# Every third modulation chunk of the attention calls sent to the buffers of the down weights

## The reference, cut to what matters

```python
for i in range(DEPTH):
    mod_lat = jax.nn.silu(c) @ w_ada[i] + b_ada[i]
    mod_ctx = jax.nn.silu(c_ctx) @ w_ada[i] + b_ada[i]
    sh1, sc1, g1, sh2, sc2, g2 = [m[:, None, :] for m in jnp.split(mod_lat, N_MOD, axis=-1)]
    ...
    attn = windowed_gqa_with_context(q, k, v, kc, vc, sink[i])
    four = fourier_mix(u, w_fourier[i])
    mix = jnp.concatenate([attn, four], axis=-1) @ w_out[i]
    x_mid = x + g1 * rmsnorm(mix, norm_post_mix[i])
    hf = modulate(rmsnorm(x_mid, norm_pre_ffn[i]), sh2, sc2)
    x = x_mid + g2 * rmsnorm(swiglu(hf, w_gate[i], w_up[i], w_down[i]), norm_post_ffn[i])
```

## Time and profile before

| what | before |
|---|---|
| median of three runs | 2457.35 us (2454.23 to 2459.2) |
| the profiled execution | 2455.65 us, its span 2453.8 us |
| PE busy, share of the span | 95% |
| chain that ended last: PE, DMA | 84%, 4% |
| mean DMA rate over the span | 160 GB/s |
| first call (latent, layer 0, 12 chunks) | 122.77 to 169.40 us |
| second call (context, layer 0, 12 chunks) | 182.10 to 225.08 us |
| third call (latent, layer 1, 14 chunks) | 740.23 to 792.21 us |

### The profile page before, as it was taken

One profiled execution on the slowest core, in us unless ns is written; L12 is line 12 of the kernel. 1 busy time (PEld: TensorE's weight loads), 2 busy tenths in 40 slices (PEclk: granted clock), 3 DMA queues, 4 the chain that ended last, 5 costly groups with the idle time before them and its releaser, 6 DMA issues.

```text
span 2453.8 us, 47218 instructions
## 1 busy us (share of the span) xinstructions
PE 2341.4 (95%) x19072; PEld 2069.9 (84%) x19072; DVE 1452.5 (59%) x2300; ACT 1031.2 (42%) x1614; POOL 301.2 (12%) x242
## 2 busy tenths in 40 slices
PE   6988999999998899999999999999999998999998
PEld 3855899899974799789998888899899888989997
DVE  1053366666625566676677654666766667555765
ACT  2153454444334433343346434533533455435433
POOL 0000000100000000000005426200000035336000
PEclk9999999999999999999999999999999998999999
DMA  6156545445426555355432223655444332125542
GB/s 273 69 206 241 192 177 181 180 181 178 148 86 241 189 189 190 115 201 189 173 120 104 87 71 123 225 184 186 170 179 181 119 137 87 70 88 183 203 179 103
DMA packets 65511, 392.50 MB, mean 160 GB/s; under 512 B 7264, under 2 KB 7392, under 8 KB 28000
## 3 DMA queue, kind: packets, MB, share of 16 engines
q1 hardware_dynamic: 64224, 383.81, 42.9%
q10 hardware_dynamic: 864, 5.17, 0.5%
q0 software_dynamic: 288, 1.57, 0.2%
HBM read 389.48 MB, written 1.05 MB: 159 GB/s over the span
## 4 chain that ended last, share of the span: by engine, by line
PE 84%; DMA 4%; DVE 4%; issue 3%; POOL 3%; ACT 2%; SPq 0%; POOLq 0%; DVEq 0%; ACTq 0%
PE ps L2118 19%; PE ps L2075 12%; PE ps L2076 11%; PE ps L2077 11%; PE ps L2120 10%; PE ps L2203 5%; DMA ring_a<-in_wa 3%; POOL t_lo L598 3%; PE ps L2218 2%; PE ps L2537 2%; PE ps L2678 1%; DMA work<-in_wa 1%; PE ps L1999 1%; PE ps L2023 1%; PE ps L2233 1%
## 5 line engine op out<-in xcount | busy, mean ns | idle before, releaser
L2118 PE MATMUL ps<-h_parts,w_hi 128*128 128x512 f32 x2000 | 711.7, 398 | 1.6 <-DVE w_lo L1341 1.6
L2120 PE MATMUL ps<-h_parts,w_lo 128*128 128x256 f32 x2000 | 561.6, 281 | 0.0
L2118 PEld LDWEIGHTS ps<-h_parts,w_hi 128*128 128x128 f32 x2000 | 376.0, 188 | 89.2 <-DVE w_lo L1341 2.4
L2120 PEld LDWEIGHTS ps<-h_parts,w_lo 128*128 128x128 f32 x2000 | 378.0, 189 | 0.0
L1341 DVE TENSOR_TENSOR w_lo<-ring_a,w_hi 128x1024 fp32r<-128x1024 f32 x308 | 363.3, 1221 | 12.7 <-ACT w_hi L692 12.5
L2075 PE MATMUL ps<-hid_hi,d_hi 128*128 128x256 f32 x1232 | 349.0, 283 | 0.0
L2076 PE MATMUL ps<-hid_lo,d_hi 128*128 128x256 f32 x1232 | 348.8, 283 | 0.0
L2077 PE MATMUL ps<-hid_hi,d_lo 128*128 128x256 f32 x1232 | 348.6, 283 | 0.0
L725 ACT ACTIVATE sg<-sg 128x256 f32<-128x256 f32 x130 | 54.4, 418 | 649.2 <-DVE sg L1396 649.2
L692 ACT CAST w_hi<-ring_a 128x1024 fp32r<-128x1024 f32 x308 | 305.6, 1040 | 7.8 <-DMA ring_a<-in_wa 7.8
L1396 DVE TENSOR_REDUCE sg<-ps 128x256 f32<-128x512 f32 x130 | 89.9, 691 | 299.9 <-PE ps L2120 299.8
(11 more groups left out here) (330 smaller groups left out, 3871.2 us busy)
## 6 DMA issues: line engine op xcount, KB each, us to landing
ring_a<-in_wa SPq DMA_DIRECT2D x282, 1024.0 KB, 4.8
ring_d<-in_wd SPq DMA_DIRECT2D x154, 512.0 KB, 5.2
work<-in_wa SPq DMA_DIRECT2D x6, 1024.0 KB, 22.3
work<-in_small POOLq DMA_DIRECT2D x2, 768.0 KB, 4.7
c<-in_c ACTq DMA_DIRECT2D x1, 1190.0 KB, 10.7
work<-in_c ACTq DMA_DIRECT2D x1, 1088.0 KB, 5.0
x<-in_x ACTq DMA_DIRECT2D x1, 1024.0 KB, 15.2
work<-in_ctx ACTq DMA_DIRECT2D x1, 1024.0 KB, 19.7
```

The costliest lines, as they stand in the source:

```text
L2118: nc.tensor.matmul(out, w_hi[:, f % 2, part, k, :], h_parts[:, k], start=(k == 0), stop=False, skip_group_check=True)
L2120: mm = nc.tensor.matmul(out[:, 1, :], w_lo[:, f % 2, part, k, :], h_hi[:, k, :], start=False, stop=(k == KD - 1), skip_group_check=True)
```

## The change

Of the chunks of `L0` and `L1`, every third one (index 2, 5, 8, ... within its group) is loaded into `ring_d`, both of its slots together, which are 1 MB; the others go through `ring_a` as before. That makes 8 of the 24 chunks of `L0` and 4 of the 14 of `L1`; the last two of `L1` stay in `ring_a`. The chunks of `ring_a` are renumbered for it. Two semaphores are added: `third_loaded` says that such a chunk has landed, `third_used` that it has been used. SP loads in the order of use: two chunks to `ring_a`, one to `ring_d`, and so on, where chunk `g` waits for the use of chunk `g - 3`. Before the first one of layer 1, SP waits until the down weights of the first two feed-forward calls have been used (`d_used` at `2 * FT`). Before the first down weights of calls 0 and 2, SP waits for the last third chunk of that layer. PE's `ada(g)` reads the chunk from `ring_d` and counts on `third_used`; ACT's `ada(b)` waits on `third_used` where the last chunk of its batch is a third one. No arithmetic changes.

```diff
@@ -307,6 +307,7 @@
         a_loaded = [sem("a_loaded0"), sem("a_loaded1")]
         d_loaded = [sem("d_loaded0"), sem("d_loaded1")]
         a_used, d_used = sem("a_used"), sem("d_used")
+        third_loaded, third_used = sem("third_loaded"), sem("third_used")
         early_loaded = [sem(f"early_loaded{i}") for i in range(ADA_EARLY)]
         x_loaded, xc_loaded, h2_part = sem("x_loaded"), sem("xc_loaded"), sem("h2_part")
         vec_loaded, c2_loaded, const_loaded, small_loaded, out_stored = (
@@ -410,6 +411,9 @@
             n += count
         assert n == LAYERS * NMOD // 2 and ada_from["M00"] >= NMOD // 2 and ada_from["B1"] >= NMOD // 2 + ADA_FIRST
 
+        in_thirds = {"adaL0": 0, "adaL1": 2 * ADA_STEP0 // 3}
+        thirds = {"adaL0": 2 * ADA_STEP0 // 3, "adaL1": ADA_STEP1 // 3}
+
         def ada_stage(name):
             return (f"ada{name}", A_ADA + ada_from[name], dict(ada_parts)[name], None)
 
@@ -430,7 +434,7 @@
         chunk0, n = {}, 0
         for name, _, count, _ in stages:
             chunk0[name] = n
-            n += count
+            n += count - thirds.get(name, 0)
 
 
         tile0, first0, n, m = {}, {}, 0, 0
@@ -453,7 +457,15 @@
 
         def ada_chunk(g):
             name = [m for m, _ in ada_parts if ada_from[m] <= g][-1]
-            return chunk0[f"ada{name}"] + g - ada_from[name]
+            i = g - ada_from[name]
+            return chunk0[f"ada{name}"] + i - ((i + 1) // 3 if f"ada{name}" in thirds else 0)
+
+        def third_chunk(g):
+            for name in in_thirds:
+                i = g - ada_from[name[3:]]
+                if 0 <= i < 3 * thirds[name] and i % 3 == 2:
+                    return in_thirds[name] + i // 3
+            return None
 
         def early_chunk(g):
 
@@ -522,8 +534,32 @@
                     sp.wait_ge(d_used, d - 1)
                 sp.dma_start(ring_d[:, slot].rearrange("p a b -> p (a b)"), src).then_inc(d_loaded[slot], 16)
 
+            def load_third(src, used):
+                if used is not None:
+                    sp.wait_ge(third_used, used)
+                sp.dma_start(ring_d[:, :].rearrange("p a b c -> p (a b c)"), src).then_inc(third_loaded, 16)
+
+            def load_thirds(name, first, count):
+                c0, n0 = chunk0[name], in_thirds[name]
+                load_a(c0, c0 % 2, wa[first])
+                load_a(c0 + 1, (c0 + 1) % 2, wa[first + 1])
+                if n0:
+                    sp.wait_ge(d_used, 2 * FT)
+                load_third(wa[first + 2], n0 or None)
+                with sp.Fori(0, thirds[name] - 1) as n:
+                    for u in range(2):
+                        load_a(n * 2 + (c0 + 2 + u), (c0 + u) % 2,
+                               wa[bass.ds(n * 3 + (first + 3 + u), 1)].rearrange("a p n -> (a p) n"))
+                    load_third(wa[bass.ds(n * 3 + (first + 5), 1)].rearrange("a p n -> (a p) n"), n + (n0 + 1))
+                for i in range(3 * thirds[name], count):
+                    c = c0 + i - thirds[name]
+                    load_a(c, c % 2, wa[first + i])
+
             for name, first, count, call in stages:
                 c0 = chunk0[name]
+                if name in in_thirds:
+                    load_thirds(name, first, count)
+                    continue
                 if call is None:
                     i = 0
                     if c0 == 0:
@@ -545,6 +581,8 @@
                 d0, dd = call * FT, ffns[call][0] * FT
                 load_a(c0, c0 % 2, wa[first])
                 load_a(c0 + 1, (c0 + 1) % 2, wa[first + 1])
+                if call in (0, 2):
+                    sp.wait_ge(third_used, in_thirds[f"adaL{call // 2}"] + thirds[f"adaL{call // 2}"])
                 load_d(d0, d0 % 2, wd[dd], wait=call > 0)
                 load_a(c0 + 2, c0 % 2, wa[first + 2])
                 load_d(d0 + 1, (d0 + 1) % 2, wd[dd + 1], wait=call > 0)
@@ -823,6 +861,8 @@
                 u, last = b % 2, BATCHES[b + 1] - 1
                 if early_chunk(last) is not None:
                     act.wait_ge(ada_early, early_chunk(last) + 1)
+                elif third_chunk(last) is not None:
+                    act.wait_ge(third_used, third_chunk(last) + 1)
                 else:
                     act.wait_ge(a_used, ada_chunk(last) + 1)
                 nc.scalar.copy(ada_rows[:, u, :], ps[:, 4 + u, 0:T]).then_inc(ada_row, 1)
@@ -1982,11 +2022,14 @@
 
             def ada(g):
 
-                b, n = batch_of(g), early_chunk(g)
+                b, n, third = batch_of(g), early_chunk(g), third_chunk(g)
                 u, i, last = b % 2, g - BATCHES[b], BATCHES[b + 1] - 1
                 if n is not None:
                     pe.wait_ge(early_loaded[n], 16)
                     tiles, done = early[:, n], ada_early
+                elif third is not None:
+                    pe.wait_ge(third_loaded, 16 * (third + 1))
+                    tiles, done = ring_d, third_used
                 else:
                     c = ada_chunk(g)
                     chunk_here(c, c % 2)
```

## The result

The changed kernel takes 2440.78 us (median of four runs, 2439.74 to 2444.25); the kernel before, with one more run beside it, 2455.84 us. The two medians are 15.1 us apart. The ratio on record is 0.9927, 95% interval 0.9915 to 0.9939: some 18 us, and by the interval 15 to 21, so the medians stand at its lower end. A second set of five runs, with its own runs of before beside it, gave 2441.14 us and 0.9929 (0.9916 to 0.9943). The forecast was 2436.0 us, 21.3 us faster; the range, 2431 to 2446, holds the result.

A forecast was written before the change was run, and what follows sets the result against it. PE's 19.9 us of waits for chunks, bound by the turnover of two buffers' slots, plus clock cost, were the stock. Savings of 3.0 + 11.3 + 7.0 = 21.3 us gave 2434.3 profiled, 2436.0 us as median; range 2431 to 2446.

The forecast's parts named there:

- Rival A: Attention calls: DMA engines deliver less than 422 GB/s; 16.1 us saved, 2441 us, or 2446 if the clock falls; chance 0.17.
- Rival B: First and third calls: softmax chain replaces the wait, they give half, 1.5 and 3.5 us; 2441 us; chance 0.06.
- the sum had 6.9: Second call, second way of reckoning: 9.1 us of waits less three staying at about 0.75 us give 6.9.
- the other 4.3 us: Second call: three low-clock stretches of about 1.45 us each vanish, 4.3 us together; lost if the clock still falls.
- First call, 3.0 forecast: First attention call: 2.04 us saved over five steps and 0.96 behind them, 3.0 us, leaving no wait for chunks.
- third call, 7.0 forecast: Third attention call: 6.10 us saved over five steps and 0.93 at 787.27, 7.0 us; supply still enough.
- the step with one chunk at 4.48 us: Latent calls: a step with one chunk lasts 4.48 us without waits, read from 144.25 to 148.73.
- The steps with two chunks: First call: a step with two chunks takes 5.45 us without waits, 5.79 less its wait of 0.34.
- Second call, 11.3 forecast: Second attention call: DMA engines become the bound; it ends at 213.8 instead of 225.08, saving 11.3 us.
- the price of a chunk, 2.49 us: Supply with three buffers: engines move 422 GB/s, so a chunk takes 2.49 us and three take 7.46.
- C: SP's in-order queue: a wait for a third chunk holds up loads behind it, 2457 us stands; chance 0.03.
- D: Instruction blocks queue behind weights on the DMA engines and stall PE; 2466 us at 3 us each; chance 0.03.

The follow-up runs named there:

- e1_floor: Changed kernel with one modulation chunk loaded per layer and used for all, 36 of 38 loads left out: 2435.95 us, ratio 0.9904.
- e2_sinks_after: Changed kernel with ACT doing exponentials and sink of the first head, then of the second, instead of both exponentials, then both sinks: 2438.32 us, ratio 0.9916.
- e4_five: Changed kernel with five chunk buffers in place of three: 2436.75 us, ratio 0.9910.
- e5_five_sinks: Changed kernel with five chunk buffers and ACT doing each head's exponentials and sink together: 2427.38 us, ratio 0.9876.
- e6_four: Changed kernel with four chunk buffers in place of three: 2434.75 us, ratio 0.9908.

## Why the prediction was right, and where its terms were off

**The bound was read rightly.** PE waited for chunks at the pace of a slot's turnover; a third buffer took that away in the first call and in part in the others, the gain lies in the three calls, and nothing behind them took it back.

**The total was nearer than its terms.** The forecast was 21.3 us; the record has 15 by the medians and 18 by the ratio. The range held because its upper end was drawn for A and B together, and something of the size of both came. And part of it is luck. In the second call the waits fell from 9.1 to 5.8 us, 3.3 us where the sum had 6.9; the other 4.3 us of the 7.6 go with the clock (PE's busy time in the call fell from 32.3 to 27.6 us), and the sum had given these on the condition that the waits be short, which they were not. Rival A had the clock fall again, for another 4.3 us, if waits of near 2 us came back.

**First call, 3.0 forecast, 0.7 to 1.0 measured; third call, 7.0 forecast, 2.3 and 4.9 measured.** The term that failed is the step with one chunk at 4.48 us; it is 5.03. It came from 144.25 to 148.73, but the step ahead of it had been stretched by a wait for a chunk, in which VectorE caught up with its normalising. Before the change VectorE then stood idle until the scores came; in the changed kernel it goes straight on to the maxima (PE and VectorE before, then VectorE after):

```profile
143.25 1.07 PE L1999 MATMUL ps<-ring_a,cs 128*32 128x256 f32 x16 [1.01 <-DMA ring_a<-in_wa]
145.41 0.30 DVE L1440 TENSOR_TENSOR ps<-ps,work 128x128 f32<-128x128 f32 x1 [0.88 <-PE ps L2259]
...
144.76 0.29 DVE L1480 TENSOR_TENSOR ps<-ps,work 128x128 f32<-128x128 f32 x1
```

Once no wait stretches the steps, the loop of 5.13 us shows, and `e1_floor` (45.6 us with nothing to wait for) and `e2_sinks_after` (43.1 us with the loop cut) show it for the first call. The steps with two chunks were put too high (5.45, measured 5.23), which hid a part: the five steps forecast at 24.34 us took 25.62. The 0.96 us to be saved behind them was not saved either, since the values now wait 1.14 us for ACT at 164.78. Rival B was this, with a price of 3.0 to 1.5 for the first call that was still too mild; the argument against it looked at steps with two chunks only. In the third call 45.7 to 45.9 us is the floor with no chunk to wait for (`e4_five`, `e1_floor`), and it falls to 43.1 with ACT's order (`e5_five_sinks`). What lies above the floor goes with late landings: waits of 3.3 us in the first profile and 1.5 in the second. The sum needed a chunk every 2.83 us there and counted on one every 2.49; the eight loads from 749.32 to 775.37 landed 3.3 us apart.

**Second call, 11.3 forecast, 7.3 to 7.6 measured.** The term that failed is the price of a chunk, 2.49 us. The engines did move at that pace, 401 GB/s from 197 to 204.5 us, but a chunk lands with its slowest engine: 2.93 us. The rate over the call was 325 GB/s, not near 370, and 363 from 205.6 to 213.4 us. Rival A had the size (some 4 us less), though not the cause; the row it took for itself, 369 GB/s by busy time or three chunks in 8.5 us, is close to the 8.71 and 8.85 measured. By the rule of the Trainium skill ("DMA: Bandwidth & Descriptors", "Where 436 GB/s comes from", some 358 GB/s for loads from HBM) a chunk would take 2.93 us, an estimate and the same number. The trace does not bear it out as a ceiling: 401 GB/s stood for 7.5 us, and `e6_four` landed chunks every 2.5 us behind 203.21. That the clock would stay at 1.00 was right in the first profile; the second had 0.95, from a low stretch at the start of the call (186 to 192 us).

**C and D** did not happen: the loads came in order, and the blocks of instructions went with loads up to 0.9 us later here and there, not with a stall of PE. The misses are 2.0 to 2.3, 3.7 to 4.0 and 2.1 to 4.7 us, some 8 to 11 by the profiles, and only 3 to 6 by the medians and ratios. A part of the difference is that the first profile of the changed kernel is 3.5 us over its median; another may be that the profile of before has short calls, but no trace of its other runs shows it.

## What to carry to other kernels

A step time read next to a wait is not the time of that step without waits: look which other engine used the wait to catch up, and follow its loop once round before a gain is counted. Two bounds of nearly the same height must be moved together: the reordering gave nothing that could be measured with two buffers, some 3 us with three, and 8 to 9 with five (by the ratios, across chips). With several loads in flight plan by the slowest DMA engine, here 2.65 to 2.93 us for 1 MB and not 2.5, or give the ring a buffer more than the mean rate asks for.

## What was not expected of the hardware

The 16 engines of a load drift apart while the queue is never empty, from 0.5 to 3.6 us between the first and the last (188.25 and 217.35 in the changed kernel), and the lag is worked off slowly if at all: with five buffers it shrank from 1.8 to 1.2 us over the loads from 203.83 to 211.37. In the first call, where the queue runs dry every few loads, it is 0.3 to 0.6 us for ten of the twelve. And the clock of TensorE fell in places without a long wait: in the kernel with five buffers PE was granted 0.54 from 186 to 189 us, behind pauses of 0.94, 0.33 and 0.22 us and short matmuls between them, and the step took 5.25 us instead of the 3.92 of the changed kernel's first profile, where the clock held through the same pauses.

```profile
183.00:186.00 3.00, 1.74 (x12) 0.86 (x16) 1.95 (x10) 1.05 (x6) 0.00 (x0) 1.00 0.66 232
186.00:189.00 3.00, 3.00 (x34) 1.26 (x26) 1.73 (x8) 1.99 (x8) 0.00 (x0) 0.54 0.53 161
```

The prediction had it only behind waits of 2 us and more. The second profile of the changed kernel fell in the same place as the one with five buffers, so the same kernel does either.
